# Gate and up products with 512 moving columns in 35 of 40 network steps, and S5 chunk-input tables made by DVE in three of those steps

## What is computed

```python
for l in range(DEPTH):
    h = rms_norm(x, ffn1_norm[l])
    x = x + 0.5 * swiglu(h, ffn1_w_gate[l], ffn1_w_up[l], ffn1_w_down[l])
    h = rms_norm(x, mix_norm[l])
    p = h @ w_in[l]
...
    x = x + mix @ w_out[l]
    h = rms_norm(x, ffn2_norm[l])
    x = x + 0.5 * swiglu(h, ffn2_w_gate[l], ffn2_w_up[l], ffn2_w_down[l])

def swiglu(x, w_gate, w_up, w_down):
    return (jax.nn.silu(x @ w_gate) * (x @ w_up)) @ w_down
```

## Time and profile before

| | us |
|---|---|
| median of 3 runs | 1032.58 (1032.25 to 1032.63) |
| the profiled execution | 1033.05 |
| its span | 1031.3 |
| TensorE busy | 1023.4, 99% of the span |
| DVE, ACT, POOL busy | 680.3, 523.5, 205.0 |
| granted TensorE clock | full in every slice |

### The profile page before, as it was taken

How to read it: one execution, slowest core, us unless ns; L and a number is a source line. 1 busy time by engine, 2 the same in 40 slices (tenths; PEclk the granted TensorE clock), 3 DMA queues, 4 the chain that set the end, 5 groups by cost and what they waited for, 6 DMA issues and landing times.

```text
span 1031.3 us, 22763 instructions
## 1 busy us (share of the span) xinstructions
PE 1023.4 (99%) x9714; PEld 1006.2 (98%) x9714; DVE 680.3 (66%) x850; ACT 523.5 (51%) x628; POOL 205.0 (20%) x291
## 2 busy tenths in 40 slices
PE   8999999999999999999999999999999999999998
PEld 7999999999899999999999999999998999999998
DVE  7666656788668555555566665668987667555554
ACT  5645434565587534343475454436456765434341
POOL 0000899800002000000020019996000020000000
PEclk9999999999999999999999999999999999999999
DMA  8746454434325464545555555453442265464541
GB/s 301 269 158 209 164 200 162 162 128 161 124 83 204 164 209 164 202 164 200 176 205 207 181 186 204 163 204 123 153 138 92 92 228 204 164 203 163 203 163 42
DMA packets 26821, 178.44 MB, mean 173 GB/s; under 512 B 3121, under 2 KB 4161, under 8 KB 5761
## 3 DMA queue, kind: packets, MB, share of 16 engines
q1 hardware_dynamic: 25632, 173.03, 47.8%
q10 hardware_dynamic: 1008, 4.05, 1.1%
q0 software_dynamic: 112, 0.40, 0.1%
HBM read 176.42 MB, written 1.05 MB: 172 GB/s over the span
## 4 chain that ended last, share of the span: by engine, by line
PE 96%; DVE 2%; DMA 1%; SPq 0%; ACT 0%; issue 0%; DVEq 0%; ACTq 0%
PE ps L815 30%; PE ps L816 30%; PE ps L817 30%; DMA raw<-stream 1%; PE ps L968 1%; PE ps L1021 1%; PE ps L1086 1%; DVE lo L1228 0%; DVE in_lo L1427 0%; PE ps L1082 0%; SPq L363 0%; PE ps L1043 0%; ACT hi L577 0%; PE ps L1062 0%; PE ps L1031 0%; PE ps L1149 0%
## 5 line engine op out<-in xcount | busy, mean ns | idle before, releaser
L1228 DVE TENSOR_TENSOR lo<-raw,hi 128x2048 fp32r<-128x2048 f32 x130 | 302.7, 2337 | 200.0 <-ACT hi L577 199.9
L815 PE MATMUL ps<-xg_hi,hi 128*128 128x256 f32 x1408 | 399.3, 284 | 2.3 <-DVE lo L1311 1.4
L816 PE MATMUL ps<-xg_lo,hi 128*128 128x256 f32 x1408 | 398.4, 283 | 0.0
L817 PE MATMUL ps<-xg_hi,lo 128*128 128x256 f32 x1408 | 398.4, 283 | 0.0
L577 ACT ACTIVATE hi<-raw 128x2048 fp32r<-128x2048 f32 x130 | 247.1, 1909 | 176.4 <-PE ps L817 170.8
L815 PEld LDWEIGHTS ps<-xg_hi,hi 128*128 128x128 f32 x1408 | 270.3, 192 | 2.9 <-issue 2.8
L816 PEld LDWEIGHTS ps<-xg_lo,hi 128*128 128x128 f32 x1408 | 270.3, 192 | 0.1
L817 PEld LDWEIGHTS ps<-xg_hi,lo 128*128 128x128 f32 x1408 | 270.3, 192 | 0.0
L815 PE MATMUL ps<-act_hi,hi 128*128 128x256 f32 x704 | 199.4, 283 | 0.6 <-DVE act_lo L1266 0.6
L816 PE MATMUL ps<-act_lo,hi 128*128 128x256 f32 x704 | 199.2, 283 | 0.0
L817 PE MATMUL ps<-act_hi,lo 128*128 128x256 f32 x704 | 199.2, 283 | 0.0
(11 more groups left out here) (317 smaller groups left out, 1339.0 us busy)
## 6 DMA issues: line engine op xcount, KB each, us to landing
raw<-stream SPq DMA_DIRECT2D x160, 1024.0 KB, 4.9
par<-params ACTq DMA_DIRECT2D x2, 1463.0 KB, 9.1
raw<-stream SPq DMA_DIRECT2D x8, 256.0 KB, 7.3
rows<-stream SPq DMA_DIRECT2D x2, 1024.0 KB, 6.9
x<-xT ACTq DMA_DIRECT2D x4, 256.0 KB, 6.6
out<-x SPq DMA_DIRECT2D x8, 128.0 KB, 2.0
con<-consts POOLq DMA_DIRECT2D x1, 371.5 KB, 6.6
mask<-masks POOLq DMA_DIRECT2D x1, 20.0 KB, 6.7
```

Source lines behind the costliest of these rows:

```text
L815: pe.matmul(acc, w_hi, a_hi, start=start, stop=False, skip_group_check=True)
L816: pe.matmul(acc, w_hi, a_lo, start=False, stop=False, skip_group_check=True)
L817: return pe.matmul(acc, w_lo, a_hi, start=False, stop=stop, skip_group_check=True)
L1228: v.tensor_tensor(lo[slot][:, :], raw[slot][:, :], hi[slot][:, :].bitcast(F32), ALU.subtract).then_inc(lo_written, 1)
```

## The change

In 35 of the 40 steps (`folded`: iterations 2 to 9 of the first network and 1 to 9 of the others) the gate and up products are made with 512 moving columns. `xg_hi` and `xg_lo` become two halves of one tile, `xg`, side by side for each k. One matmul with the hi weights streams both, 512 columns, into a whole bank: the left half gets hi x hi, the right half hi x lo. A second one with the lo weights adds lo x `xg_hi` into the left half. So there are two matmuls and two weight loads for the same 768 columns. Gate then takes banks 6, 7 and up banks 4, 5, in every folded iteration; there is no second set.

The halves have to be added afterwards. ACT copies the right half of gate into `silu` and that of up into `act` (both free at this time); DVE adds the left halves to them into `gate` and `up`, and then multiplies each by `rstd` in two more operations. `gu_read` is now counted one higher, so that a step begins when the iteration just finished has been read; in the first step of networks 2 to 4 only up waits for this. The first iterations and the last stay with 256 columns.

Second, `w_lag` is made by DVE: ten operations behind the splits of iteration 5 and six behind those of 6 and 7, in the first network of each layer, and not by POOL at the end of its list. TensorE's `s5_input` waits for the new `lags_ready`.

```diff
+            def folded(f, i):
+                return 0 < i < ITERS - 1 and (f > 0 or i > 1)
...
@@ on ACT
                 def gated(i, odd, after_silu=lambda: None, first=False):
+                    if folded(f, i):
+                        e.wait_ge(units_done, n0 + i * 3 + 1 + RING)
+                        e.wait_ge(act_lo_ready, f * ITERS + i)
+                        for b, rest in ((6, silu), (4, act)):
+                            e.activation(rest[:, :, :], bank(b, 2).rearrange("p (m s t) -> p m s t", m=2, s=2)[:, :, 1, :],
+                                         ACT.Copy).then_inc(rest_copied, 1)
...
@@ on TensorE
+                            b = 6 - 2 * half + m
+                            pe.matmul(bank(b), hi[slot][:, w:w + P], xg[:, k, :, :].rearrange("p s t -> p (s t)"),
+                                      start=k == 0, stop=False, skip_group_check=True)
+                            last = pe.matmul(bank(b)[:, 0:T], lo[slot][:, w:w + P], xg_hi[:, k, :],
+                                             start=False, stop=k == KT - 1, skip_group_check=True)
...
-                    pe.wait_ge(gu_read, f * ITERS + i + 1)
-                    gate_up(0, n, 2, 4 + 2 * g, lambda: row_sums(norm, False, 3) if head and first else None)
-                    gate_up(1, n + 1, 0, 4 + 2 * g)
+                    pe.wait_ge(gu_read, f * ITERS + i + (1 if first else 2))
+                    gate_up(0, n, 2, wide, lambda: row_sums(norm, False, 3) if head and first else None)
+                    if first and wide:
+                        pe.wait_ge(gu_read, f * ITERS + i + 2)
+                    gate_up(1, n + 1, 0, wide)
...
@@ on DVE
+                    v.wait_ge(rest_copied, folds(f, i) * 2 - 1)
+                    v.tensor_tensor(gate[:, :, :], of_gate[:, :, 0, :], silu[:, :, :], ALU.add
+                                    ).then_inc(gate_summed, 1)
+                    v.wait_ge(rest_copied, folds(f, i) * 2)
+                    v.tensor_tensor(up[:, :, :], of_up[:, :, 0, :], act[:, :, :], ALU.add).then_inc(gu_read, 1)
+                    v.wait_ge(gate_summed, folds(f, i))
+                    v.tensor_tensor(gate[:, :, :], gate[:, :, :], wide, ALU.mult).then_inc(gate_scaled, 1)
+                    v.wait_ge(gu_read, f * ITERS + i + 2)
+                    v.tensor_tensor(up[:, :, :], up[:, :, :], wide, ALU.mult).then_inc(up_scaled, 1)
...
-                ffn_steps(l * 2, l * SPLIT_UNITS, l * 3, False, {2: angles, 4: coefficients})
+                ffn_steps(l * 2, l * SPLIT_UNITS, l * 3, False,
+                          {2: angles, 4: coefficients, 5: lambda: lag_power(2), 6: lambda: lag_power(1),
+                           7: lambda: lag_power(0)})
```

More of the change, by code:

```diff
@@ L353, in build, with folds @@
         mix_hgrn = sem("mix_hgrn")
+        def folded(f, i):
+            return 0 < i < ITERS - 1 and (f > 0 or i > 1)
+        def folds(f, i):
+            return sum(folded(g, j) for g in range(f + 1) for j in range(ITERS if g < f else i + 1))
         block = ctx.enter_context(nc.Block())
@@ L518, in _ @@
                         last.then_inc(tables_ready, 1)
[L521 to L545, removed]
                 steps.close()
@@ L852, in ffn, with gate_up @@
                 last.then_inc(units_done, 2)
-                def gate_up(half, n, slot, b, between=lambda: None):
+                def gate_up(half, n, slot, wide, between=lambda: None):
                     pe.wait_ge(lo_written, n + 1 + RING)
@@ L860, in gate_up, with step @@
                             w = k * 256 + m * P
[L861 to L863 removed]
+                            if not wide:
+                                last = three(bank(6 + m)[:, half * T:(half + 1) * T], hi[slot][:, w:w + P],
+                                             lo[slot][:, w:w + P], xg_hi[:, k, :], xg_lo[:, k, :],
+                                             k == 0, k == KT - 1)
+                                continue
+                            b = 6 - 2 * half + m
[3 more added lines that the diff above has]
+                                             start=False, stop=k == KT - 1, skip_group_check=True)
                     last.then_inc(units_done, 1)
[L866 removed]
+                def step(i, g, first=False, wide=True):
                     n = n0 + i * 3 + 2
[L869 to L871 removed]
+                    pe.wait_ge(gu_read, f * ITERS + i + (1 if first else 2))
[3 more added lines that the diff above has]
+                    gate_up(1, n + 1, 0, wide)
                     pe.wait_ge(lo_written, n + 3 + RING)
@@ L880, in step @@
                     last.then_inc(units_done, 1)
-                step(0, 1, True)
+                step(0, 1, True, folded(f, 1))
                 with pe.Fori(0, (ITERS - 3) // 2) as ii:
@@ L1408, in coefficients, with lag_power @@
                                     ).then_inc(forget_ready, 1)
-                ffn_steps(l * 2, l * SPLIT_UNITS, l * 3, False, {2: angles, 4: coefficients})
+                def lag_power(lag):
+                    row = lambda i: rows[:, i, :]
+                    if lag == LAG - 2:
+                        v.wait_ge(row_funs, l * 3 + 3)
+                        st.mark(v.tensor_tensor(row(3), row(3), row(3), ALU.mult))
+                        st.wait()
+                        st.mark(v.tensor_scalar(row(3), row(3), -2.0, 1.0, ALU.mult, ALU.add))
+                        st.wait()
+                        st.mark(v.tensor_tensor(row(4), row(0), row(3), ALU.mult))
+                        st.mark(v.tensor_tensor(row(5), row(0), row(2), ALU.mult))
+                        b_re, b_im = prm("b_re"), prm("b_im")
+                    else:
+                        b_re, b_im = w_lag[:, lag + 1, 0, :], w_lag[:, lag + 1, 1, :]
+                    o_re, o_im = w_lag[:, lag, 0, :], w_lag[:, lag, 1, :]
+                    st.wait()
+                    v.tensor_tensor(o_re, b_re, row(4), ALU.mult)
+                    v.tensor_tensor(row(6), b_im, row(5), ALU.mult)
+                    v.tensor_tensor(o_im, b_im, row(4), ALU.mult)
+                    st.mark(v.tensor_tensor(row(7), b_re, row(5), ALU.mult))
+                    st.wait()
+                    v.tensor_tensor(o_re, o_re, row(6), ALU.subtract)
+                    last = v.tensor_tensor(o_im, o_im, row(7), ALU.add)
+                    if lag:
+                        st.mark(last)
+                    else:
+                        last.then_inc(lags_ready, 1)
+                ffn_steps(l * 2, l * SPLIT_UNITS, l * 3, False,
+                          {2: angles, 4: coefficients, 5: lambda: lag_power(2), 6: lambda: lag_power(1),
+                           7: lambda: lag_power(0)})
                 def wait_ffn1(m):
```

34 lines of the change are left out of this document (21 added, 13 removed).

## The result

| | before | the change |
|---|---|---|
| median of 15 runs, us | 1032.72 (1032.23 to 1033.12) | 1034.78 (1032.75 to 1036.08) |
| ratio, 95% interval | | 1.002 (1.0012 to 1.0027) |
| profiled execution, its span | 1033.05, 1031.3 | 1034.78, 1032.7 |
| TensorE matmuls | 9714 | 8594 |
| DVE, ACT, POOL busy | 680.3, 523.5, 205.0 | 740.6, 558.0, 167.4 |

The change took 1,120 matmuls and their weight loads away and made the kernel 2.1 us slower, on the edge of what can be told. The forecast was 1021, with a range from 1006 to 1029.

A forecast was written before the change was run, and what follows sets the result against it. TensorE's own pace was taken to bound the kernel. 12.3 us saved less 0.6 lost in first steps gave 11.7; from 1032.58 that made 1020.9, say 1021. Its own range was 1015 to 1026.5, with rivals 1006 to 1029.

The forecast's parts named there:

- The tables on DVE: 22 table operations in iterations 5 to 7, both layers: 3.8, 2.3 and 2.3 us, covered by spare, costing TensorE nothing.
- What bounds the kernel: Whole kernel: TensorE, busy 99% of the span, sets the end by its own pace; a step is 17.28 us.
- The saving of a place: Gate and up products: 512 plus 256 columns take 0.349 us, saving 0.011 (0.007 to 0.017) in 1,120 places, 12.3 us.
- I take that it does: Gate and up products: assumed that the 256-column matmul with lo weights keeps 0.120 us behind a wider one.
- The fast weight load's 13.3 ns: Cross-check of the saving: a weight load of 32 cycles, 13.3 ns, would make a place 0.347 us and save 14.9 us.
- Banks, slot 0, slot 2 in a plain step: Folded step: added ACT and DVE work costs nothing; spare 3.8 us for banks, 2.6 for slot 0, slot 2 refilled in time.
- The rival on the slower side: Slot 0's weights come after gate's products if the chain grows over 2.6 us; 1056 with 1 us beyond; chance 0.07.
- the mixed case: Steps 4 to 7 or slot 0 run out of spare, stalls eating part of the gain: 1026.5 to 1031; chance 0.08.
- under 0.5 us a step: Limit put on the stalls in steps 4 to 7 or at slot 0 when they eat part of the gain.
- POOL would have been late by 0.3 us or more: End of the first network: tables left on POOL would delay its sums of squares by 0.3 us or more.
- First steps of networks 2 to 4: First folded step there: up starts some 0.2 us late for its banks; 0.2 each, 0.6 us lost in all.

The follow-up runs named there:

- e7: The change with lag tables in iterations 5, 9 and 9, and in each m eight 512-column matmuls, then eight of 256, instead of alternating: 1024.68 us, ratio 0.992.
- e5: The kernel before with 168 more warm-up matmuls on zeros, 24 each of seven forms, to time their pace; 512 columns of fp32r took 0.227 us.
- e4: The change without POOL's output tables (c_out set to zero once), lag tables still on DVE in iterations 5, 6, 7: 1026.78 us, ratio 0.9942.
- e1: The change with its folded products, but the lag tables back on POOL as in the kernel before: 1032.59 us, ratio 0.9999.

## Why the prediction was wrong

Two terms of the sum failed. The tables on DVE were put at nothing ("So nothing reaches PE"); beside POOL's work and in folded steps they cost 8.1 us of waits and lower clock (4.8 and 3.3, around iteration 8 of networks 1 and 3), and turned the sign. And the saving on TensorE was put at 12.3 us and came to 7.4.

- *What bounds the kernel: right.* TensorE's pace sets the end, and each us that it was held is in the result.
- *The saving of a place: two thirds too large, and just outside the lower end.* It was to be 0.011 (0.007 to 0.017); it is 0.0067, 7.4 us and not 12.3. The step that failed is "I take that it does": no row showed a 256-column matmul behind a wider one, and I priced the two forms as if each stood among its like. Among their like my values nearly hold, 0.230 and 0.119 (e7). Alternating, they cost 0.353 and not 0.349. The lower end of my range has a slip too: 1032.6 - 19.0 + 0.6 is 1014, not 1015.
- *The fast weight load's 13.3 ns:* it describes 256, 384 and 512 columns in a row (e5), though not the run with 32 weight columns, and it did not help with the pair. In the Trainium skill (TensorE: Matmul & The Clock Gate, section on weight-path perf modes) the 32 cycles are a theoretical value for fp8, and the fast load is off for FP32 inputs; I had left this out. Whether fp32r uses it no run here tells.
- *Banks, slot 0, slot 2 in a plain step: right.* With POOL quiet no plain step waits. From the first copy to the end of slot 0's lo the chain runs as worked out: 371.59 to about 380.5 by the trace, 8.9 against 8.7.
- *The tables on DVE: this is where the sign turned.* The text costs 22 operations at 0.34 to 0.45 each, from rows in which POOL was idle (68.31), and puts POOL's effect at 0.75 for each of two splits in iteration 7 alone. In the trace of the change the operations follow each other after 0.34 to 0.45 in iteration 5, as costed, after 0.55 in iteration 6 (134.50, 135.05) and after 0.75 in iteration 7, all three splits end late there, and the lag of 4.4 us is followed by scales of 1.05 and 1.23. The step's spare of 2.6 us and that of the banks, 3.8, were both overrun. In the kernel before, DVE had no 128x256 work at this time, so the row to take was POOL's own: its w_lag and c_out operations, 0.61 to 0.64 alone, took 2.7 beside a split of DVE's (timeline of POOL, kernel before; the splits run from 176.76 and from 179.60):

```profile
176.57 0.64 POOL L535 TENSOR_TENSOR rows<-par,rows 128x256 f32<-128x256 f32 x1
177.17 2.69 POOL L536 TENSOR_TENSOR w_lag<-par,rows 128x256 f32<-128x256 f32 x1
```

I read this as POOL's problem alone. I also forgot that a scale that once read PSUM now reads two SBUF tensors: the reads out of PSUM kept their 0.68 at 158.06, the scales behind them did not. The Trainium skill (GPSIMD Engine Reference, Specifications) says that POOL shares its SBUF interface with VectorE, with contention where a DVE instruction has two SBUF inputs; the trace agrees, with 0.83 against 0.41 (e4) for just such operations and 0.68 for those with one input in PSUM. Had I applied that to the table of iteration 7, six times 0.4 more, the lag in the forecast would have been 1.8 + 2.4 = 4.2 us, above the spare of 2.6, and the wait would have been in it.

- *The rival on the slower side* was the right mechanism at the wrong scale: slot 0 and the banks, from a chain more than 2.6 us longer. I priced it as if in all 35 steps, 1056, and gave it a chance of 0.07. It happened in two steps, and the mixed case, a pace gain with a handful of late steps, was given 1026.5 at best and 1031 at worst. Its cap, "under 0.5 us a step", had no row behind it.
- *The clock had no term.* A wait of 2.17 us was followed by 3.4 us at 1.2 GHz, worth another 1.6 us, in one network of the profiled execution.
- *POOL would have been late by 0.3 us or more:* right in kind; e1 shows 2.0 us at TensorE. POOL's whole list of table operations takes 96.3 us there (103.96 to 200.3) and 91.9 in the kernel before (105.24 to 197.2), so I had also left out that POOL slows; that DVE's added work is what slows it is likely, not shown.
- *First steps of networks 2 to 4:* a forecast of 0.6 us in all; the waits there are 0.8 us in three places by PE's weight loads, right.

## What to carry to other kernels

Price work that is moved to another engine from rows in which the engine it leaves, or its neighbour, is as busy as it will be then, and look for operands that change from PSUM to SBUF. A chain that has room in the average step has to be laid out for the worst step, since a few late steps can give back a gain that was made in 35. Time a new instruction among the neighbours that it will have: two forms of matmul in turn cost 1% more here than the same ones in groups of eight (0.353 against 0.350), and regrouping them gained 3.5 us, about half of what the folding gained.

## What was unexpected of the hardware

- fp32r matmuls with zeros: 0.227 for 512 columns, 0.174 for 384, 0.119 for 256, 0.110 for 128; bf16 0.216 and 0.109. With 32 weight columns instead of 128, 512 columns took 0.231, more and not less.
- 512 and 256 columns in turn take 0.353 a pair, in a pattern that repeats every three pairs; two and two 0.348; eight and eight in the network 0.350; the sum of each alone 0.347. The cause of the difference is open.
- Whether the lower clock followed a wait differed: in the profiled executions it did after 2.17 us in network 1 of the change and after 2.0 us in both of e1, and did not after 2.06 us in network 3 of the change, nor after the two waits of 0.75. Among the runs of one kernel it differed too: three of fifteen kept the full clock throughout in the change, five of eleven in e1. What decides was not tried.
- POOL and DVE slow each other: 128x256 operations on two SBUF inputs take 0.83 instead of 0.42 on DVE beside POOL's, and 2.7 instead of 0.6 on POOL beside a DVE split of 128x2048; DVE reads with one input in PSUM keep their 0.68.
